# Gate-up as Strassen groups: seven half-token block products for eight, with GpSimd summing the weight blocks

## The reference

```python
h = rms_norm(x, norm_ffn_pre[l])
f = (jax.nn.silu(h @ w_gate[l]) * (h @ w_up[l])) @ w_down[l]
x = x + rms_norm(f, norm_ffn_post[l])
```

## Time and profile before

| | us |
|---|---|
| median of 3 runs | 1160.26 (1159.33 to 1161.4) |
| span of the profiled execution | 1158.6 |
| TensorE matmul busy in it | 1131.8 |
| VectorE busy | 642.0 |
| ScalarE busy | 498.3 |
| GpSimd busy | 121.3 |

### The profile page before, as it was taken

The page is one execution under the profiler, slowest core; times in us unless marked ns, Lnnn a source line. Parts: engine busy times, 40 slices in busy tenths (PEclk is TensorE's granted clock), DMA queues, the critical chain, the costliest instruction groups (busy, mean ns, idle before and its releaser), DMA issues.

```text
span 1158.6 us, 15494 instructions
## 1 busy us (share of the span) xinstructions
PE 1131.8 (98%) x5560; PEld 936.1 (81%) x5560; DVE 642.0 (55%) x1071; ACT 498.3 (43%) x853; POOL 121.3 (10%) x143
## 2 busy tenths in 40 slices
PE   8999989999999999999999999999999999999997
PEld 6788777988888888888898887787888888888886
DVE  6888986766444444333278588473544444433333
ACT  6887874544223223222265458453332232232321
POOL 1576742000000000000000004200000000000000
PEclk9999999999999999999999999999999999999999
DMA  7323313214222222322313220032322322322212
GB/s 273 121 64 83 91 38 127 92 56 134 93 99 96 94 99 94 106 102 98 109 65 109 91 91 2 19 110 77 122 92 91 105 93 92 106 93 98 102 55 73
DMA packets 34114, 108.81 MB, mean 94 GB/s; under 512 B 4368, under 2 KB 7056, under 8 KB 33936
## 3 DMA queue, kind: packets, MB, share of 16 engines
q1 hardware_dynamic: 33312, 107.22, 27.3%
q10 hardware_dynamic: 752, 0.92, 0.3%
HBM read 100.78 MB, written 2.10 MB: 89 GB/s over the span
## 4 chain that ended last, share of the span: by engine, by line
PE 88%; DVE 5%; ACT 3%; issue 1%; POOL 1%; DMA 1%; ACTq 0%; SPq 0%; DVEq 0%; POOLq 0%
PE bank L505 24%; PE bank L507 24%; PE bank L506 24%; PE bank L1022 2%; PE bank L1012 2%; PE bank L967 1%; PE bank L1095 1%; PE bank L968 1%; PE bank L969 1%; PE bank L1097 1%; PE bank L1096 1%; DVE wl L426 1%; PE bank L2056 1%; PE bank L2054 1%; PE bank L2055 1%
## 5 line engine op out<-in xcount | busy, mean ns | idle before, releaser
L426 DVE TENSOR_TENSOR wl<-raw,wh 128x1024 fp32r<-128x1024 f32 x181 | 223.5, 1236 | 299.7 <-ACT wh L418 299.6
L418 ACT ACTIVATE wh<-raw 128x1024 fp32r<-128x1024 f32 x181 | 191.1, 1058 | 421.3 <-PE bank L507 275.1
L505 PE MATMUL bank<-hh,wh 128*128 128x512 f32 x872 | 343.7, 394 | 2.8 <-DVE wl L426 1.4
L507 PE MATMUL bank<-hh,wl 128*128 128x512 f32 x872 | 339.8, 390 | 0.0
L506 PE MATMUL bank<-hl,wh 128*128 128x512 f32 x872 | 339.6, 389 | 0.0
L505 PEld LDWEIGHTS bank<-hh,wh 128*128 128x128 f32 x872 | 163.7, 188 | 40.1 <-issue 3.3
L506 PEld LDWEIGHTS bank<-hl,wh 128*128 128x128 f32 x872 | 163.8, 188 | 35.0 <-issue 1.7
L507 PEld LDWEIGHTS bank<-hh,wl 128*128 128x128 f32 x872 | 163.7, 188 | 34.4
L507 PE MATMUL bank<-gh,wl 128*128 128x512 f32 x308 | 121.7, 395 | 0.0
L505 PE MATMUL bank<-gh,wh 128*128 128x512 f32 x308 | 121.7, 395 | 0.0
L506 PE MATMUL bank<-gl,wh 128*128 128x512 f32 x308 | 121.7, 395 | 0.0
(11 more groups left out here) (251 smaller groups left out, 1627.7 us busy)
## 6 DMA issues: line engine op xcount, KB each, us to landing
raw<-weights SPq DMA_DIRECT2D x181, 512.0 KB, 3.2
xres<-x_t SPq DMA_DIRECT2D x8, 512.0 KB, 6.1
sw<-ta SPq DMA_DIRECT2D x36, 64.0 KB, 2.0
out_t<-final SPq DMA_DIRECT2D x6, 256.0 KB, 2.5
q<-sw SPq DMA_DIRECT2D x10, 128.0 KB, 2.3
q<-ta SPq DMA_DIRECT2D x10, 128.0 KB, 2.3
rope<-angles SPq DMA_DIRECT2D x1, 1024.0 KB, 11.3
sw<-ta ACTq DMA_DIRECT2D x4, 64.0 KB, 3.0
```

The lines of the kernel that those rows point to most:

```text
L418: act.activation(wh[:, j, :, :], raw[:, j, :, :], ACT.Copy).then_inc(high_split, 1)
L426: v.tensor_tensor(wl[:, j, :, :], raw[:, j, :, :], wh[:, j, :, :].bitcast(F32), ALU.subtract)\
L505: pe.matmul(bank[:, :], wh[:, slot, b, :], ah[:, k, :], start=first and n == 0, stop=False)
L507: ins = pe.matmul(bank[:, :], wl[:, slot, b, :], ah[:, k, :], start=False, stop=last and n == len(blocks) - 1)
```

## The change

The first 6 of the 22 tiles of each gate-up (PLAIN) stay as they are. Each of the 16 others is a group. The weights of its gate and up tile are taken as a 2 x 2 block matrix: gate and up are the rows, the two halves of the 1024 input features the columns. The activations are 2 x 2 as well: halves of the features by halves of the tokens. Their product, four blocks of 128 features by 256 tokens, is made by Strassen's scheme in Winograd's form: seven products of blocks instead of eight. A block product is 4 x 3 matmuls of 256 columns (`seven` in `pe_group`), 84 matmuls a group where two chunks had 48 of 512.

Each of the seven products has a weight unit of half a chunk (512 elements a partition): P1, P2 and P4 a block as it is, P5, P6, P3 and P7 sums or differences, which GpSimd makes (`gpsimd_weight_sum`) into `wsum`, which shares its place with `wl`. ScalarE makes the high part of every unit (`act_unit`), VectorE the low part (`vec_unit`), in a ring of eight half slots. A slot is free again when TensorE has multiplied the unit eight before it.

Each of the seven has a token operand too, `h7`, made once for each gate-up while the plain tiles run: ScalarE scales x by the gain into four blocks (`act_tokens`, four instructions each), GpSimd multiplies them by rstd and makes four differences (`gpsimd_tokens`), ScalarE and VectorE make the high and low parts of the seven (`act_seven`, `vec_seven`, 1024 elements a partition each). rstd is then already in the operand.

The four outputs of a group are put together from four PSUM banks. P1 and P2 add up in bank A, P5 and P3 in C, P6 and P7 in B, P4 in D. ScalarE copies P1 and P5 aside (`act_keep`) before P2 and P3 are added on top; VectorE makes the joins (`vec_join_x`, `vec_gate_second`, `vec_join_u`, `vec_up_first`, 256 elements each, one input in PSUM), GpSimd one of 256 (`gpsimd_upper`), ScalarE silu in two halves (`act_gated`). `taken`, `joined` and `upper` count them, and TensorE waits for some of them.

The token operands lie in the arena where gh and gl of tiles 8 to 21 belong, so the split of these tiles is put off: their products are kept whole in `gwhole` (in the place of hh and hl) and split in the last group and at the start of down. gh and gl of a tile now lie beside each other. Down waits for the low parts tile by tile in its first output tile. The loops are written out; semaphores are shared by the two gate-ups (`Tally`, `reached`).

The diff, cut to its core:

```diff
-PHASES = [("in1", len(IN1), 1, len(IN1)), ("out1", KT, 1, len(UNITS)), ("gu1", 2 * FT, 1, 2 * FT), ("down1", KT, len(DOWN), KT + 1),
-          ("in2", len(IN2), 1, len(IN2)), ("out2", KT, 1, KT), ("gu2", 2 * FT, 1, 2 * FT), ("down2", KT, len(DOWN), KT + 1)]
+PLAIN = 6
+GROUPS = FT - PLAIN
+EARLY_SPLIT = 8
+HK = KT // 2
+PHASES = [("in1", len(IN1), 1, len(IN1)), ("out1", KT, 1, len(UNITS)), ("gu1", 2 * FT, 1, 2 * PLAIN), ("down1", KT, len(DOWN), KT + 1),
+          ("in2", len(IN2), 1, len(IN2)), ("out2", KT, 1, KT), ("gu2", 2 * FT, 1, 2 * PLAIN), ("down2", KT, len(DOWN), KT + 1)]
...
+P1, P5, P6, P2, P3, P7, P4 = range(7)
+SUM_AT = {P5: 1, P6: 2, P3: 3, P7: 4}
...
+LOW7 = {P1: 1, P5: 2, P3: 3, P7: 4, P6: 5, P2: 6, P4: 7}
...
         wl = place("wl", [P, RING, CH, P], F32R)
+        wsum = place("wsum", [P, RING, CH, P], at=wl_at)
         turn_at = top[0]
         ta = place("ta", [P, 2, S])
...
-        gl = place("gl", [P, FT, S], F32R, at=arena + 44 * KB)
+        gsplit = place("gsplit", [P, FT, 2, S], F32R, at=arena)
+        gh, gl = gsplit[:, :, 0, :], gsplit[:, :, 1, :]
+        gwhole = place("gwhole", [P, FT - EARLY_SPLIT, S], at=hh_at)
+        h7 = place("h7", [P, 7, 2, HK, S // 2], F32R, at=arena + 4 * EARLY_SPLIT * KB)
...
         def pe_gate_up(pe, gu, norm, n_added=None):
-            for j in range(4):
-                pe.wait_ge(low_split, gu.c0 + 4 + j + 1)
-                if j == 3:
+            for j in range(4, 2 * PLAIN):
+                slot_wait(pe, gu.c0 + j)
+                if j == 7:
                     pe.wait_ge(norm.ready, 1)
-                products(pe, banks[4 + j], (gu.c0 + j) % RING, range(KT), hh, hl, 0, True, True).then_inc(used, 1)
-                if j == 0 and n_added is not None:
+                if j >= 8:
+                    bank_free(pe, gu.t0 + j)
+                products(pe, banks[4 + j % 4], (gu.c0 + j) % RING, range(KT), hh, hl, 0, True, True).then_inc(used, 1)
+                if j == 4 and n_added is not None:
                     sum_squares(pe, norm, n_added, acc, banks[7])
-            with pe.Fori(2, FT // 2) as i:
-                for j in range(4):
-                    pe.wait_ge(low_split, 4 * i + gu.c0 + j + 1)
-                    bank_free(pe, gu.t0 + j, i)
...
+        def pe_group(pe, gu, m):
+            def seven(bank, p, first):
+                q = half_slot(gu, 7 * m + p)
+                reached(pe, gu.unit_low, 7 * m + p + 1)
+                if m == 0:
+                    reached(pe, gu.seven_low, LOW7[p])
+                j, b = q
+                o = bank[:, 0:S // 2]
+                for k in range(HK):
+                    wk = b.start + k
+                    pe.matmul(o, wh[:, j, wk, :], h7[:, p, 0, k, :], start=first and k == 0, stop=False, skip_group_check=True)
+                    pe.matmul(o, wh[:, j, wk, :], h7[:, p, 1, k, :], start=False, stop=False, skip_group_check=True)
+                    ins = pe.matmul(o, wl[:, j, wk, :], h7[:, p, 0, k, :], start=False, stop=k == HK - 1, skip_group_check=True)
+                ins.then_inc(gu.multiplied.of, 1)
+            a, c, b, d = (group_bank(m, i) for i in (BANK_A, BANK_C, BANK_B, BANK_D))
+            if m == 1:
+                pe.wait_ge(bank_read, gu.t0 + 2 * PLAIN)
+            if m >= 2:
+                reached(pe, gu.taken, 4 * (m - 2) + 3)
+            seven(a, P1, True)
+            if m >= 2:
+                reached(pe, gu.joined, 4 * (m - 2) + 2)
+            seven(c, P5, True)
+            if m >= 2:
+                reached(pe, gu.joined, 4 * (m - 2) + 3)
+            seven(b, P6, True)
+            reached(pe, gu.taken, 4 * m + 1)
+            seven(a, P2, False)
+            reached(pe, gu.taken, 4 * m + 2)
+            seven(c, P3, False)
+            reached(pe, gu.joined, 4 * m + 1)
+            seven(b, P7, False)
+            if m >= 2:
+                reached(pe, gu.joined, 4 * (m - 2) + 4)
+            seven(d, P4, True)
+        kept1, kept5 = acc[:, 0:S // 2], acc[:, S // 2:S]
+        join_x, join_u = rh[:, 0:S // 2], rh[:, S // 2:S]
...
+            o = wsum[:, j, b, :]
+            if p == P5:
+                weights_landed(g, gu, m, 0)
+                weights_landed(g, gu, m, 1)
+                ins = g.tensor_tensor(o, weight_block(gu, m, 1, 0), weight_block(gu, m, 1, 1), ALU.add)
+            elif p == P6:
+                reached(g, gu.summed, 8 + 4 * m + 1)
+                ins = g.tensor_tensor(o, unit_source(gu, m, P5), weight_block(gu, m, 0, 0), ALU.subtract)
+            elif p == P3:
+                reached(g, gu.summed, 8 + 4 * m + 2)
+                ins = g.tensor_tensor(o, weight_block(gu, m, 0, 1), unit_source(gu, m, P6), ALU.subtract)
+            else:
+                ins = g.tensor_tensor(o, weight_block(gu, m, 0, 0), weight_block(gu, m, 1, 0), ALU.subtract)
+            ins.then_inc(gu.summed.of, 1)
...
+        def gpsimd_upper(g, gu, m):
+            f = PLAIN + m
+            reached(g, gu.joined, 4 * m + 3)
+            reached(g, gu.taken, 4 * m + 2)
+            reached(g, gu.product, f - 1)
+            g.tensor_tensor(sw[:, f % 2, S // 2:S], join_u, kept5, ALU.add).then_inc(gu.upper.of, 1)
...
+            sum_of("t1", "12", "11", 2)
+            scale("22")
+            sum_of("t2", "22", "t1", 4)
+            sum_of("t3", "22", "12", 4)
+            scale("21")
+            sum_of("t4", "21", "t2", 7)
+        def gpsimd_gate_up(g, gu, norm):
+            gpsimd_tokens(g, gu, norm)
+            for m in range(-1, GROUPS):
+                if m + 1 < GROUPS:
+                    for p in (P5, P6, P3, P7):
+                        gpsimd_weight_sum(g, gu, m + 1, p)
+                if m >= 0:
+                    gpsimd_upper(g, gu, m)
...
+        def vec_unit(v, gu, m, p):
+            if m >= GROUPS:
+                return
+            j, b = half_slot(gu, 7 * m + p)
+            reached(v, gu.unit_high, 7 * m + p + 1)
+            if p in FREED_BY_SUM:
+                reached(v, gu.summed, 8 + 4 * m + FREED_BY_SUM[p])
+            v.tensor_tensor(wl[:, j, b, :], unit_source(gu, m, p), wh[:, j, b, :].bitcast(F32), ALU.subtract).then_inc(gu.unit_low.of, 1)
...
         def vec_gate_up(v, gu, norm):
             v.wait_ge(norm.ready, 1)
-            for r in range(2):
-                vec_gate(v, gu, r, banks[(gu.t0 + 2 * r) % 4], banks[(gu.t0 + 2 * r + 1) % 4])
-                vec_product(v, gu, r)
-                vec_split(v, gu.c0 + RING + r + 2)
-                vec_hidden_low(v, gu, r)
-            vec_split(v, gu.c0 + RING + 4)
-            with v.Fori(1, FT // 2) as i:
-                for r in range(2):
-                    vec_gate(v, gu, r, banks[4 + 2 * r], banks[5 + 2 * r], i)
-                    vec_product(v, gu, r, i)
-                    vec_split(v, gu.c0 + RING + 2 * r + 1, i)
-                    vec_hidden_low(v, gu, r, i)
-                    vec_split(v, gu.c0 + RING + 2 * r + 2, i)
...
-        down_half = {name: sem(name + "_first_half") for name in ("down1", "down2")}
+            for f in range(PLAIN - 1):
+                vec_gate(v, gu, f)
+                vec_product(v, gu, f)
+                for c in {0: (6,), 1: (7, 8), 2: (9, 10), 3: (11,)}.get(f, ()):
+                    vec_split(v, gu.c0 + c)
+                vec_hidden_low(v, gu, f)
+                if f == 2:
+                    vec_seven(v, gu, P1, 3)
+                    vec_seven(v, gu, P5, 5)
+                if f == 3:
+                    vec_unit(v, gu, 0, P1)
+                    vec_seven(v, gu, P3, 6)
+                    vec_seven(v, gu, P7, 6)
+                    vec_unit(v, gu, 0, P5)
+            vec_unit(v, gu, 0, P6)
+            vec_unit(v, gu, 0, P2)
+            vec_seven(v, gu, P6, 8)
+            vec_seven(v, gu, P2, 8)
+            vec_unit(v, gu, 0, P3)
+            vec_unit(v, gu, 0, P7)
+            vec_seven(v, gu, P4, 8)
+            f = PLAIN - 1
+            vec_gate(v, gu, f)
+            vec_unit(v, gu, 0, P4)
+            vec_product(v, gu, f)
+            vec_hidden_low(v, gu, f)
+            for m in range(GROUPS - 1):
+                vec_group(v, gu, m)
...
+        def vec_group(v, gu, m):
+            f = PLAIN + m - 1
+            if m:
+                vec_up_first(v, gu, m - 1)
+            vec_unit(v, gu, m + 1, P1)
+            if m:
+                vec_group_product(v, gu, m - 1)
+            vec_unit(v, gu, m + 1, P5)
+            if m and f < EARLY_SPLIT:
+                vec_hidden_low(v, gu, f)
+            vec_join_x(v, gu, m)
+            vec_gate_second(v, gu, m)
+            vec_unit(v, gu, m + 1, P6)
+            vec_unit(v, gu, m + 1, P2)
+            vec_join_u(v, gu, m)
+            vec_unit(v, gu, m + 1, P3)
+            vec_unit(v, gu, m + 1, P7)
+            vec_unit(v, gu, m + 1, P4)
...
+        def act_tokens(act, gu, gain, what):
+            row, n = int(what[0]) - 1, HALVES[int(what[1]) - 1]
+            for k in range(HK):
```

(57 more changed lines are left out.)

334 lines of the change are left out of this document (243 added, 91 removed).

## The result

The changed kernel takes 1187.6 us (median of 4 runs, 1187.2 to 1188.2) against 1159.8 for the kernel before on the same chip: a ratio of 1.0239, 95% interval 1.0225 to 1.0254. It is 27.8 us slower; 11 were forecast. The profiled execution spans 1186.2 us, 27.6 more than before.

The account below looks back on a forecast made before the run. TensorE was taken to bound gate-up. Late group 0s (22.4 + 13.5) less 17.6 gained in the loop gave +18.3 alternating; 15 + 6.5 - 17.6 gave +3.9 VectorE first; half way +11, 1171 us, range 1142 to 1187.

Parts of the forecast that it names:

- Exclusion: VectorE's two-SBUF-input work and GpSimd's work exclude each other; a 512-element GpSimd operation blocks VectorE some 1.10 us.
- The layout by hand: Before group 0, VectorE's and ScalarE's queues laid out instruction by instruction, to find how late group 0 ends.
- the alternating order: Before group 0, VectorE and GpSimd take turns; group 0 ends 22.4 and 13.5 us behind, +18.3 in all.
- VectorE first: Before group 0, VectorE's two-input operations pass waiting GpSimd ones; 15 and 6.5 us behind, +3.9 in all.
- bank B's join: In steady groups, the join needed before P7, behind the third weight sum, comes 0 to 0.7 us late every few groups.
- Rival 1: Exclusion costs little, GpSimd's operations falling into VectorE's waits for ScalarE; 1140, or 1150 with the loop at 10.4; chance 0.22.
- rival 2: Exclusion partly cheap, or TensorE-bound groups after a costly start before group 0; -12 to +4 us, 1148 to 1164; chance 0.18.
- Rival 3: Group loop becomes the bound: sums blocking 1.5 us give 11.7 a group, +60; at 1.25, +30; chance 0.10.
- The gap formula: TensorE: N/2.4 + 2.5 ns between matmuls gives pair 10.4, group 9.2, gain 1.2 us; trace starts disagree.

Follow-up runs that it names:

- the cuts: GpSimd's gate-up operations in the changed kernel cut to 8 elements: all of them 1135.65 us, only the token work 1163.2, only the weight sums and join 1158.9.

## Why the prediction was right in its direction and short in its size

**The mechanism held.** Exclusion was read from two encounters and a price of 1.10 us for each GpSimd operation of 512. Without GpSimd's work the time is 52 us shorter, the token part and the weight part adding up. The waits were where the prediction looked for them: P5 and P6 of group 0 waited 3.4 and 4.0 us (3 to 6 foreseen), P2 4.3 (5 to 9 foreseen, a little less) with `act_keep` as releaser. Splits of 1024 took up to 3.4 us (3.3 foreseen); groups 3 to 15 averaged 10.35, within 10.1 to 10.5.

**The layout by hand held.** In the alternating order it had `vec_gate` 3 end at 287.1 and `vec_gate` 4 at 304.0; their last readings start at 286.36 and 303.41 and last 0.68. VectorE was to lose 19.4 us; its operations with two SBUF inputs that start between 252 and 317 took 19.6 longer than undisturbed (the six splits 2.86 us on average for 1.23, the six low parts of hidden tiles 1.42 for 0.69, the seven of tokens 1.52 for 1.22, the eight units 1.09 for 0.69). Group 0 was to end at 323.8 and ended at 325.56; in gate-up 2 it was to end 13.5 us behind, measured 14.8. TensorE's own part held too: a group without a wait takes 9.97 us (10.08 from 0.120, and 0.119 was the lower bound).

**The step that failed is the sum.** It had +18.3 for the alternating layout and +3.9 for "VectorE first", argued for the first, and then took the middle, +11. The trace shows strict turns (5.91 us for two splits). Halving took away 7.3 us that the prediction had already worked out; two values of which one is true have no middle that is. The other 9.3 us, from +18.3 to the measured +27.6, are terms of the alternating case itself (the rows below, each rounded, add up to it within 0.2):

| term | forecast, us | measured, us | difference |
|---|---|---|---|
| group 0 late, gate-up 1 | 22.4 | 24.2 (325.56 - 301.4) | +1.8 |
| group 0 late, gate-up 2 | 13.5 | 14.8 (895.51 - 861.8 - 18.9 from gate-up 1) | +1.3 |
| groups 1 to 15, both (163.3 plain) | 2 x 154.5 | 158.1 + 157.8 | +6.9 |
| after down 2 | 0 | -0.5 | -0.5 |

- **Groups 1 and 2** took 11.7 in both gate-ups where 10.3 was taken for all: 4 x 1.4 = 5.6 of the 6.9. Part of this is a missed term: the high and low parts of tiles 6 and 7 stand in these two groups alone, and the prediction counted a group's work by the general case. Moving these parts back in their group took 1.7 and 1.6 us off group 1 of the two gate-ups. Group 2 kept its time, with the wait at P7 that every third group has, so the other 2.3 us are not shown to come from the parts. Without GpSimd's weight sums both groups take 9.97.
- **Groups 3 to 15** average 10.35 (134.6 / 13) against 10.3 and hold the other 1.2 in both gate-ups. The wait is the one that was named, bank B's join ahead of P7 behind the third sum, each third group. Timeline of GpSimd, VectorE and TensorE in such a group:

```profile
403.64 1.55 POOL L2087 TENSOR_TENSOR wsum<-wsum,raw 128x512 f32<-128x512 f32 x1
403.97 0.41 DVE L2212 TENSOR_TENSOR sw<-bank,rh 128x256 f32<-128x256 f32 x1
404.31 1.44 DVE L2183 TENSOR_TENSOR wl<-raw,wh 128x512 fp32r<-128x512 f32 x1
405.67 0.68 DVE L2165 TENSOR_TENSOR gwhole<-ta,sw 128x512 f32<-128x512 f32 x1
406.12 1.37 POOL L2090 TENSOR_TENSOR wsum<-raw,wsum 128x512 f32<-128x512 f32 x1 [0.93 <-PE bank L2048]
406.27 1.77 DVE L2183 TENSOR_TENSOR wl<-wsum,wh 128x512 fp32r<-128x512 f32 x1
407.96 0.41 DVE L2196 TENSOR_TENSOR rh<-bank,acc 128x256 f32<-128x256 f32 x1
408.43 0.39 PE L2046 MATMUL bank<-h,wh 128*128 128x256 f32 x1 [0.97 <-DVE rh L2196]
```

  The low part issued 0.15 us behind the third sum takes 1.77, and the join behind it comes 0.97 too late. VectorE has no idle time ahead of the join in this stretch; at the undisturbed 0.68 the low part alone would have brought the join 1.1 us sooner (an estimate from these rows), which is more than the wait. At 403.97 a VectorE operation with one input in PSUM keeps its 0.41 beside GpSimd. The section cited ahead of the forecast (the Trainium skill, SBUF — State Buffer, section "Who interferes with whom") agrees with both: whoever issues first has the shared ports for its whole instruction, and a VectorE instruction with at most one SBUF input does not contend in this way.
- **Group 0's tail.** The keep came 1.0 us earlier than laid out (P2 starts at 317.06 against 318.1), but P2 to P4 then took 8.50 us and not 5.76: TensorE's granted clock was at its half level (0.50), a cost that the prediction put at nothing (last section). In gate-up 2 the same: P2 1.5 us early, 2.8 us lost behind it.

**The range and the rivals.** 1187.6 lies just above the range's 1187. The alternating case as laid out gives 1160.26 + 18.3 = 1178.6, which left 8.4 us below the upper end for anything missed; 9.3 were missed. Rival 1 (exclusion costs little) is refuted by the cuts. Of rival 2 the costly way in came, but not its loop at TensorE's own rate. Rival 3 (a loop above 10.89) did not come: only groups 1 and 2 and every third one are above it. The gap formula that the prediction set beside the measured starts stands in the Trainium skill (TensorE: Matmul & The Clock Gate, section "Back-to-back issue gap") for a matmul by itself, not for a stream; no term of the sum used it.

## What to carry to other kernels

Before work moves to GpSimd beside a VectorE whose queue of two-SBUF-input operations has little room (66% full here without GpSimd's work), price it as VectorE time: here up to 1.1 us for each operation of 512 elements and up to 2.1 for 1024. In the loop it came to 3.2 us a group, still more than the 2.6 that VectorE needed to do the same work itself. A way into a new schedule is to be laid out queue by queue, as here, with the items that only the first two or three rounds have, and where it doesn't fit beside the work at hand, start the new schedule a step later; reordering alone only moved the waits here. Where two mechanisms are possible and one is argued for, the forecast takes its number, and the other belongs in the range.
